# A three-headed attention layer in float32: the memory keys and values made before stick-breaking, and two of its projections moved by a few steps

## The reference

```python
h = rmsnorm(x, g_pre);  p = h @ w_in          # columns split among the heads
y_A = stick_breaking(8 heads of 64) * silu(gate_A)     # strictly causal
y_B = differential_attention(4 heads) * silu(gate_B)   # block-causal, partial rotary
mkv = rmsnorm(mem, g_mem) @ w_mem_kv          # 256 x 512: keys and values of 4 heads
y_M = softmax(mq @ mk.T / 8) @ mv * silu(gate_M)       # cross-attention
x   = x + rmsnorm(concat(y_A, y_B, y_M) @ w_out, g_post)
```

## Time and profile before

| | us |
|---|---|
| median of 3 runs | 2056.37 (2056.11 to 2059.1) |
| the profiled execution | 2055.35 |
| its span, first to last instruction | 2053.6 |
| busy in the span: TensorE, its weight loads | 1873.9 (91%), 1579.8 (77%) |
| VectorE, ScalarE, GpSimd | 1306.2 (64%), 1083.0 (53%), 604.1 (29%) |
| granted TensorE clock, mean over the span | 0.945 of 2.4 GHz |

### The profile page before, as it was taken

How to read it: one execution, slowest core, us unless ns; L and a number is a source line. 1 busy time by engine, 2 the same in 40 slices (tenths; PEclk the granted TensorE clock), 3 DMA queues, 4 the chain that set the end, 5 groups by cost and what they waited for, 6 DMA issues and landing times.

```text
span 2053.6 us, 34304 instructions
## 1 busy us (share of the span) xinstructions
PE 1873.9 (91%) x11552; PEld 1579.8 (77%) x11552; DVE 1306.2 (64%) x2685; ACT 1083.0 (53%) x2406; POOL 604.1 (29%) x542
## 2 busy tenths in 40 slices
PE   6999998899999999999999959999788999989998
PEld 6999998678787878787878857777566666767886
DVE  7705887577777777777676832434477788754444
ACT  6321211566666666666666722433378989962221
POOL 0000000344444444444444500101145666650000
PEclk9999999999999999999999868999689999998999
DMA  6432113000010101010101021424710404016542
GB/s 217 105 72 62 66 66 108 13 8 25 7 25 6 26 5 26 5 26 5 26 5 26 4 75 56 130 74 131 169 28 16 98 18 99 7 39 234 181 144 82
DMA packets 121867, 129.29 MB, mean 63 GB/s; under 512 B 81936, under 2 KB 94992, under 8 KB 120464
## 3 DMA queue, kind: packets, MB, share of 16 engines
q1 hardware_dynamic: 121744, 127.86, 21.5%
HBM read 85.89 MB, written 41.94 MB: 62 GB/s over the span
## 4 chain that ended last, share of the span: by engine, by line
PE 68%; DVE 15%; issue 7%; ACT 5%; DMA 2%; POOL 2%; SPq 0%; DVEq 0%; POOLq 0%; ACTq 0%
PE ps L662 8%; PE ps L648 6%; PE ps L616 5%; PE ps L617 5%; PE ps L618 5%; PE ps L603 4%; PE ps L604 4%; PE ps L605 4%; DVE small L1503 4%; PE ps L896 3%; PE ps L897 3%; PE ps L898 3%; PE ps L636 2%; PE ps L637 2%; DVE ring L1363 2%
## 5 line engine op out<-in xcount | busy, mean ns | idle before, releaser
L1621 POOL TENSOR_TENSOR ring_r<-ring,sp_hi 128x512 fp32r<-128x512 f32 (+1 forms) x320 | 358.5, 1120 | 822.4 <-DVE sp_hi L1366 822.4
L662 PEld LDWEIGHTS ps<-v,ring 128*128 128x128 f32 x2176 | 298.8, 200 | 55.4 <-DVE acc L1383 22.8
L662 PE MATMUL ps<-v,ring 128*128 128x65 f32 x2176 | 298.2, 279 | 16.5 <-DVE acc L1383 10.2
L1009 ACT ACTIVATE ring<-ps 128x512 f32<-128x512 f32 (+1 forms) x320 | 170.5, 533 | 221.6 <-PE ps L637 165.6
L1363 DVE SCALAR_TENSOR_TENSOR ring<-ring,ps 128x512 f32<-128x512 f32 (+1 forms) x320 | 192.0, 600 | 34.8 <-ACT ring L1014 32.8
L603 PE MATMUL ps<-w_hl,ht_hi 128*128 128x256 f32 x768 | 213.5, 278 | 0.7 <-DVE w_hl L1244 0.6
L604 PE MATMUL ps<-w_hl,ht_hi 128*128 128x256 f32 x768 | 213.3, 278 | 0.0
L605 PE MATMUL ps<-w_hl,ht_lo 128*128 128x256 f32 x768 | 213.3, 278 | 0.0
L616 PE MATMUL ps<-ht_hi,w_hl 128*128 128x512 f32 x448 | 200.0, 446 | 13.3 <-DVE ring L1351 7.0
L1647 POOL TENSOR_TENSOR p<-p 128x1024 f32<-128x1024 f32 (+4 forms) x96 | 164.9, 1729 | 159.5 <-ACT p L1156 159.2
L1021 ACT ACTIVATE ring<-ps 128x512 f32<-128x512 f32 (+1 forms) x320 | 170.3, 532 | 60.5 <-PE ps L648 59.7
(11 more groups left out here) (186 smaller groups left out, 3954.3 us busy)
## 6 DMA issues: line engine op xcount, KB each, us to landing
w_raw<-in_w_narrow SPq DMA_DIRECT2D x18, 512.0 KB, 3.9
xb<-in_x SPq DMA_DIRECT2D x16, 512.0 KB, 4.1
gate_scr<-ring SPq DMA_DIRECT2D x64, 128.0 KB, 1.8
qk_scr<-w_hl SPq DMA_DIRECT2D x32, 256.0 KB, 3.4
gb<-gate_scr SPq DMA_DIRECT2D x16, 512.0 KB, 3.8
yb<-y_scr SPq DMA_DIRECT2D x16, 512.0 KB, 4.7
xr<-in_x SPq DMA_DIRECT2D x16, 512.0 KB, 4.3
out_y<-ob SPq DMA_DIRECT2D x16, 512.0 KB, 2.9
```

The costliest lines, as they stand in the source:

```text
L662: mm = pe.matmul(ps[:, 4 + i % 2, j * (HD + 1):(j + 1) * (HD + 1)], ring[:, 4 + i % 2, j * P:(j + 1) * P], v1[:, kb, :], start=True, stop= ...
L1621: nc.gpsimd.tensor_tensor(ring_r[:, i % 4, j0 * P:], ring[:, i % 4, j0 * P:], sp_hi[:, i % 4, j0 * P:].bitcast(F32), ALU.subtract).then_in ...
```

## The change

The memory stage stands between the gates and stick-breaking. The order of narrow chunks becomes: four of the memory, eight of stick-breaking, then the rest. `mem_h`, `mem_g`, `mt_hi`, `mt_lo` get tiles of their own in the region that the sine and cosine tables and stick-breaking use at other times; the results `km_hi`, `km_lo` and `vm` lie in the unused halves of `w_hl` and `w_raw` and stay there through stick-breaking; the rotary buffers `hi_tmp`, `lo_tmp` and the cosines move out of those halves.

- SyncE: the two stores of the sine tables come before the gates' loop. After the first narrow weights are asked for (last gate chunk), `mem_g` and both tiles of `mem` are asked for together. The other three memory chunks and the first of stick-breaking follow behind the last gate store.
- ScalarE: both squares ahead of the exponential of pair 3 of the last gate chunk, both root chains ahead of pair 5.
- VectorE: both variances ahead of pair 4, both Newton chains and scalings ahead of pair 6.
- TensorE: the 16 transposes behind the last gate matmuls, into banks 0-3, when the gates of pair 3 are through; keys and values behind the last gate product, into banks 4 to 7, 0 and 1. Stick-breaking waits for all copies of them.
- After stick-breaking the first projection waits for the stacking counts of the last head, the second for its last accumulation.
- In stick-breaking two projections start earlier, the copies have a slot of their own in the table, and the splits start at slot 12.

```diff
-SB_PROJECT = ((0, 2, 3), (0, 3, 13), (1, 0, 24), (1, 1, 34), (1, 2, 43))
-SB_SPLIT = 16
+SB_PROJECT = ((0, 2, 3, 7), (0, 3, 10, 14), (1, 0, 20, 28), (1, 1, 34, 38), (1, 2, 43, 47))
+SB_SPLIT = 12
```

```diff
 @sync
             sp.wait_ge(w_lo_ok, C_MK * DC)
             sp.dma_start(w_raw_n, w_narrow[0]).then_inc(w_raw_in, 16)
+            sp.wait_ge(trig_out, 32)
+            sp.dma_start(mem_g[:], g_mem.broadcast_to((P, D))).then_inc(mm_in, 16)
+            for b in range(2):
+                sp.dma_start(mem_h[:, b, :], mem[b * P:(b + 1) * P, :]).then_inc(mm_in, 16)
             store_gates(N_G - 1)
+            for c in range(C_MK, C_SB):
+                sp.wait_ge(w_lo_ok, (c + 1) * DC)
+                sp.dma_start(w_raw_n, w_narrow[c + 1 - C_MK]).then_inc(w_raw_in, 16)
```

```diff
 @scalar
+            def mem_squares():
+                act.wait_ge(mm_in, 48)
+                for b in range(2):
+                    nc.scalar.activation(mem_sq[:], mem_h[:, b, :], ACT.Square, accum_out=col(0, b)).then_inc(mm_sq, 1)
+                    act.wait_ge(mm_sq, b + 1)
...
+                    if cols == NARROW and b == 3:
+                        mem_squares()
+                    if cols == NARROW and b == 5:
+                        for q in range(2):
+                            rsqrt_of(col(1, q), col(2, q), col(3, q), mm_var, q + 1, mm_ln, mm_y0)
```

```diff
 @vector
+                    if cols == NARROW and b == 4:
+                        for q in range(2):
+                            dve.wait_ge(mm_sq, q + 1)
+                            nc.vector.tensor_scalar(col(1, q), col(0, q), 1.0 / D, EPS, ALU.mult, ALU.add).then_inc(mm_var, 1)
+                    if cols == NARROW and b == 6:
+                        for q in range(2):
+                            dve.wait_ge(mm_y0, q + 1)
+                            newton(col(1, q), col(3, q), col(4, q), col(5, q), mm_ch, 4 * q)
+                            nc.vector.scalar_tensor_tensor(out=mem_h[:, q, :], in0=mem_h[:, q, :], scalar=col(5, q), in1=mem_g[:],
+                                                           op0=ALU.mult, op1=ALU.mult).then_inc(mm_h, 1)
```

```diff
 @tensor
+            pe.wait_ge(vg_ok, 8 * (N_V + N_G + 1) - 4)
+            for b in range(2):
+                pe.wait_ge(mm_h, b + 1)
+                for dc in range(DC):
+                    mm = pe.transpose(ps[:, 2 * b + dc // 4, (dc % 4) * P:(dc % 4 + 1) * P], mem_h[:, b, dc * P:(dc + 1) * P], ident[:])
+                mm.then_inc(mm_ps, 1)
             pe.wait_ge(vg_ok, 8 * (N_V + N_G + 1))
+            pe.wait_ge(mm_lo, 4)
+            for k in range(4):
...
+            pe.wait_ge(mm_ka, 4)
+            pe.wait_ge(mm_kd, 2)
```

More of the change, by code:

```diff
@@ L53 @@
 N_V, N_G = V_W // WIDE, D // WIDE
-C_SB = N_V + N_G
-C_MK = C_SB + SB_H
-C_X = C_MK + 4
+C_MK = N_V + N_G
+C_SB = C_MK + 4
+C_X = C_SB + SB_H
 NEG = -1e30
@@ L413, in _ @@
             sp.wait_ge(sb_acc, 1 + SB_H * N_ST)
[L414 to L420, removed]
+            sp.wait_ge(w_lo_ok, (C_X + 1) * DC)
+            sp.dma_start(w_raw_n, w_narrow[C_X + 1 - C_MK]).then_inc(w_raw_in, 16)
             def load_cos_sin(f):
@@ L695, in _ @@
                 sb_slot(SB_H - 1, i, False)
[L698 to L726, removed]
             def x_project(e):
+                if e == 1:
+                    pe.wait_ge(sb_acc, 1 + SB_H * N_ST)
                 if e >= 2:
@@ L1001, in _ @@
             gates(N_G - 1, NARROW)
+            for b in range(2):
+                act.wait_ge(mm_ps, b + 1)
+                for g in range(2):
+                    nc.scalar.activation(mt_hi[:, 4 * g:4 * g + 4, b * P:(b + 1) * P],
+                                         ps[:, 2 * b + g, :].rearrange("p (c s) -> p c s", c=4), ACT.Copy).then_inc(mm_hi, 1)
+            for k in range(4):
+                for dc in range(DC):
+                    split_hi(C_MK + k + 1, NARROW, dc, (mm_kv, k + 1))
+                act.wait_ge(mm_kv, k + 1)
+                if k < 2:
+                    nc.scalar.activation(km_hi[:, k, :], ps[:, 4 + k, 0:NMEM], ACT.Copy).then_inc(mm_ka, 1)
+                else:
+                    b0 = (6, 0)[k - 2]
+                    nc.scalar.activation(vm[:, :, (k - 2) * P:(k - 1) * P], ps[:, b0:b0 + 2, 0:P], ACT.Copy).then_inc(mm_ka, 1)
             def sb_exp_z(h, i):
@@ L1037, in sb_slot @@
                     sb_exp_w(h, i - 3)
-                for ahead, n, at in SB_PROJECT:
-                    if at + 4 <= i < at + 6 and (more or not ahead):
-                        for k in (0, 1) if i == at + 4 else (2,):
+                for ahead, n, at, stack in SB_PROJECT:
+                    if stack <= i < stack + 2 and (more or not ahead):
+                        for k in (0, 1) if i == stack else (2,):
                             sb_stack_hi(h, ahead * NT + n, k)
@@ L1355, in _ @@
             gates(N_G - 1, NARROW)
+            for b in range(2):
+                for g in range(2):
+                    dve.wait_ge(mm_hi, 2 * b + g + 1)
+                    rows = (slice(None), slice(4 * g, 4 * g + 4), slice(b * P, (b + 1) * P))
+                    nc.vector.tensor_tensor(mt_lo[rows], ps[:, 2 * b + g, :].rearrange("p (c s) -> p c s", c=4),
+                                            mt_hi[rows].bitcast(F32), ALU.subtract).then_inc(mm_lo, 1)
+            for k in range(4):
+                for dc in range(DC):
+                    split_lo(C_MK + k + 1, NARROW, dc)
+                if k < 2:
+                    dve.wait_ge(mm_ka, k + 1)
+                    nc.vector.tensor_tensor(km_lo[:, k, :], ps[:, 4 + k, 0:NMEM], km_hi[:, k, :].bitcast(F32), ALU.subtract).then_inc(mm_kd, 1)
+            dve.wait_ge(mm_kv, 4)
             def sb_softplus(h, i):
@@ L1400, in sb_slot @@
                     sb_softplus(h, i - 1)
-                for ahead, n, at in SB_PROJECT:
-                    if at + 5 <= i < at + 7 and (more or not ahead):
-                        sb_stack_lo(h, ahead * NT + n, i - at - 5)
+                for ahead, n, at, stack in SB_PROJECT:
+                    if stack < i <= stack + 2 and (more or not ahead):
+                        sb_stack_lo(h, ahead * NT + n, i - stack - 1)
                 if SB_SPLIT < i <= SB_SPLIT + DC:
@@ L1707, in head @@
         return np.concatenate([part[q][:, h * HD:(h + 1) * HD], part[k][:, h * HD:(h + 1) * HD]], axis=1)
-    narrow = [head("sb_q", "sb_k", h) for h in range(SB_H)]
-    narrow += [kv[:, c * P:(c + 1) * P] for c in range(4)]
+    narrow = [kv[:, c * P:(c + 1) * P] for c in range(4)]
+    narrow += [head("sb_q", "sb_k", h) for h in range(SB_H)]
     narrow += [part["m_q"][:, k * P:(k + 1) * P] if kind == "m" else head("df_q", "df_k", k)
```

109 lines of the change are left out of this document (43 added, 66 removed).

## The result

The changed kernel took 2034.44 us (median of 4 runs, 2028.52 to 2035.85), against 2057.73 for the kernel before on the same chip: 0.9883 of it, interval 0.9866 to 0.99. Run again later it took 2029.51 (5 runs, 2027.25 to 2034.62), again 0.9883 (0.9865 to 0.9902). So it is faster by 1.2%, 23 to 27 us, where 50 were forecast. The result lies inside the stated range of 1994 to 2044, and near the 2036 of rival 1. The profiled execution took 2035.85, its span 2034.1, the mean clock 0.960 (0.945 before).

A forecast was written before the change was run, and what follows sets the result against it. TensorE, on the chain that ended last for 68% of a 2053.6 us span, was taken as the bound. Moving the memory stage (-22) and earlier projections and splits (-28) took 2056.4 to 2006 us; range 1994 to 2044.

The forecast's parts named there:

- rival 1: Stick-breaking: the clock fall stays once a head, moved to steps 18-22; total 2036 us; chance 0.33.
- Part 1: Memory stage moved from behind stick-breaking to between gates and stick-breaking: net -22.0 us (-31 to -18).
- The gain at the old place: Behind stick-breaking: the memory stage's 56.1 us go, and 2.5 from a full-clock first projection; 58.6 us.
- The price at the new place: Between gates and stick-breaking: the moved memory stage delays the first projection there; 36.6 us.
- Rival 3: Memory stage: its values run at full clock; 9 us less, about 1997 us; chance 0.07.
- Rival 4: Last gate chunk: it waits for the `mem` loads; 5.5 to 10 us come back, about 2013 us; chance 0.07.
- Part 2: Stick-breaking: earlier projections and splits save 3.8 us a looped head and 1.5 in the last; -28 us.
- Steps 9-12, new: Stick-breaking, per head: stalls fall beside projection quarters, so the loss drops from 1.6 to 0.4 us.
- a stall that stays: Start of stick-breaking: TensorE's 3.53 us stall between the two first projections remains unchanged.
- the fall of steps 22 to 25: Stick-breaking: the old half-clock stretch, costing 4.4 us a head, was expected to go.
- The sign of being wrong in part 2: Looped heads of stick-breaking: clock 0.50 in any stretch, or a head of 102 or more; then 2036 or 2067.
- Rival 2: Stick-breaking: a second clock fall at about step 32 besides 19, 4.4 us a head; 2067 us; chance 0.11.

The follow-up runs named there:

- mem_only: Changed kernel with the old projection table (3, 13, 24, 34, 43) and splits from slot 16, so only the memory stage moves; 2029.06 us, repeated 2031.7.
- after: The changed kernel itself, with the memory stage moved and projections at steps 10 and 20, against the kernel before; 2034.44 us, 0.9883.
- at2: Changed kernel with the tile before the step 10 projection projected at 2 and stacked at 6 (next head's third tile 42, 46); 1999.1 us.
- at11: Changed kernel with the projection at step 10 put one slot later, at 11, and its copies at 15; 1996.37 us.
- second_at24: Changed kernel with the projection at step 10 put at 11 (copies at 15) and the one at 20 back at 24; 2003.35 us.
- steps11_only: Kernel before, memory stage at its old place, with projections at steps 3, 11, 20, 34, 43 and splits from 12; 2018.19 us.
- at12: Changed kernel with the projection at step 10 put at 12, its copies at 16 and splits from 13; 1996.35 us.
- pad8: Changed kernel with GpSimd's two zero fills of 32 x 4096 in the cross stage cut into eight of 32 x 1024; 2030.66 us.
- after_again: The changed kernel run once more, unchanged; 2029.51 us, 0.9883 of the kernel before.

## Why the prediction was wrong, point by point

**Part 1: right.** Keys at 359.08 (forecast 358), TensorE idle 9.35 us before them (8 to 10), first score at 408.36 (409), one weight wait of 2.24 (2.2). The gain at the old place: from the last values matmul to the first matmul of the cross stage (L758 before, L759 after) 69.98 us before and 11.42 in mem_only, so 58.56 (58.6 forecast). The price at the new place, from the end of the gates to the first score, rose by 34.3 in after and 34.7 in mem_only (36.6 forecast). That gives 24; the medians give 28 and 25 for mem_only in its two batches. Rival 3 held for 1.4 us only: the values ran at full clock to 370.8 and at half behind it. Rival 4 did not come: no wait for `mem` stands in the chain.

**Part 2: wrong, and in one step,** "Steps 9-12, new: their stalls fall beside quarters. Loss 0.4." The loss there was 5.0: 17.57 us against 12.6 of own work and quarters (7.0 + 5.6). Of it 2.40 are the wait for bank 7, 0.54 the wait for `ring` ahead of it, and most of the rest the matmuls of 0.63 us instead of 0.40 until 742.8. at2 has the same quarters in these steps and the one wait down to 0.22: there they take 13.38, 4.2 less, and steps 13 to 33 take as long as in after (49.63 and 49.59). at11 moves one quarter out of steps 9 to 12, so it compares over steps 9 to 33: again 4.2 less (62.92 and 67.16). Over the eight heads of the profiled executions that is 33 us for at11 and 31 for at2 (the heads sum to 801.8 in after, 768.5 in at11, 770.8 in at2), which is all of the difference to the later runs of the changed kernel; the other 5 us of the 38 are the difference between its two series of runs. The step named VectorE's lag but not what a projection waits for before its first matmul: that the last reader of its bank is done. With the stacking of the first tile left at 7 and the projection moved from 13 to 10, the distance from L1417 (slot 9 both times) to the projection shrank from four slots to one. Table and code tell that ahead of any run, and a row did too: the 3.53 us of the earlier trace rows, which the prediction took over as a stall that stays, is this same wait for `sb_s` ahead of a projection into bank 7.

**The clock: right where it was argued, wrong where it was not looked for.** The forecast said that the fall of steps 22 to 25 goes and that none comes in the ten steps without projection. Both held: steps 13 to 33 took 49.6 us against 50.0 forecast, at a clock of 1.00. Rival 1 gave nearly the right time, 2036, by another mechanism: it moved the old fall to steps 18 to 22. What came was a fall at step 10, behind a wait that no part of the text had at that place. That the cost of it, and so the time, came out near rival 1's was luck. The sign of being wrong in part 2 (0.50 in any stretch of a looped head) did come, by a cause that the text did not name. The fall that went was worth 4.9 a head (steps 19 to 33 take 43.4 in mem_only and 38.6 in second_at24, with the same quarters), 4.4 by the forecast; the wait that came, with the half clock behind it, made steps 9 to 12 take 4.6 more than forecast (17.57 - 13.0). Rival 2 did not come.

**Reason for the old fall: half right.** The prediction gave the credit to both moves. second_at24 shows that moving the first projection, its stacking and the splits does it without the second projection's move.

**The sum.** Part 1 gave -25 to -28 where -22 were forecast. Part 2 gave -6.5 by itself, and on top of part 1 +5 in one pair of medians and -2 in the other, where -28 were forecast. Together -23 to -27 for -50. With the one slot mended (at2, at11) the measured change is -55 to -61, more than forecast: a looped head is 4.7 us shorter in at11 (102.40 to 97.70) where 3.8 were forecast.

The trace of after shows the fall behind a wait of 2.40 us, that of steps11_only behind one of 1.40, and that of before behind one of 1.05, each among other short waits (and one of 1.40, as shown, brought none). The Trainium skill, "TensorE: Matmul & The Clock Gate", section "Why this matters for your kernels", ties a drop in mid-kernel to a single gap between bursts, longer than any of these three; by it the wait of 2.40 would have cost its own length and no half clock behind it. The traces disagree with it, and agree with the section on micro-idles that the prediction cited.

## What to carry to other kernels

When an order table moves a producer, list for it not only its inputs but the last reader of the buffer that it writes, and count the slots between the two before and after; a reader that itself waits for a third engine (here ScalarE's copy, then VectorE's own queue) needed two slots here, not one: with two the wait was 0.2 to 0.3 us at steps 10 and 11 and 0.74 at step 20 of at12, with one 2.4. In this loop the wait of 2.4 us cost 4.2, because TensorE went on at half clock behind it. And before a difference of 5 us in 2030 is explained, run both kernels again beside each other.

## What the runs showed of the hardware

**A fill of GpSimd holds an instruction of VectorE to its end.** VectorE's timeline and GpSimd's in after: the scaling of two columns (L1476) starts at 1426.42 during the first fill and ends at 1432.54, when the second fill does (1429.01 + 3.51); the reciprocal behind it ends with it. Without a fill beside it the scaling takes 0.17 (the last row below).

```profile
1426.42 6.12 DVE L1476 TENSOR_SCALAR small<-small 128x2 f32<-128x2 f32 x1
1427.30 5.24 DVE L1482 RECIPROCAL small<-small 128x2 f32<-128x2 f32 x1
```
```profile
1425.56 3.51 POOL L1641 MEMSET df_q<- 32x4096 f32 x1
1429.01 3.51 POOL L1641 MEMSET df_k<- 32x4096 f32 x1
```

In mem_only the same instruction ends at 1427.10, when the first fill does (begun at 1423.6):

```profile
1424.42 2.68 DVE L1476 TENSOR_SCALAR small<-small 128x2 f32<-128x2 f32 x1
```
With the fills in pieces of 0.9 us (pad8) none is held longer than 0.99:

```profile
1420.17 0.99 DVE L1476 TENSOR_SCALAR small<-small 128x2 f32<-128x2 f32 x1
...
1426.71 0.17 DVE L1476 TENSOR_SCALAR small<-small 128x2 f32<-128x2 f32 x1
```

Which of two lengths the hold has, 2.7 or 6.1 us, isn't set by the kernel: after_again is after once more, and its hold took 2.67. That it ends with a fill is shown. The Trainium skill, "SBUF — State Buffer", section "Who interferes with whom", says that VectorE's scalar form can take the port pair it shares with GpSimd, and that whoever comes second is blocked for the whole instruction of the other. The traces agree where the hold is 2.7 us, and with the fills cut it is short; that a hold runs on through a second fill is seen in the one trace of after. In the ten other profiled executions with uncut fills (before and the other runs but pad8) it took 2.44 to 2.68. TensorE waited 5.77 us for what followed in after, and 2.33 in mem_only and after_again. So the long hold is rare among the profiled executions, and it is part of why after's took 2035.85. That cutting the fills showed no gain in the medians (pad8 and after_again are within their spread) leaves open whether the cross stage takes up the usual hold.

**The clock stayed at half for 18 us of nearly full work** (370.8 to 389.0 above), with matmuls of 128 columns, as it had at the old place (TensorE busy 20.50 of 20.50 us at 0.50 there, 1217.6 to 1238.1). No run here changed their shape, so whether another one would bring the clock back wasn't tried.
